# Recurrent chunks as a software pipeline: half levels of two directions in alternation, the neighbours' products between them

## The reference

```python
def step(S, inp):
    w_t, k_t, v_t, a_t, b_t = inp[-5:]
    sa = jnp.einsum('bhvk,bhk->bhv', S, a_t)
    S = S * w_t[:, :, None, :] + sa[..., None] * b_t[:, :, None, :] + v_t[..., None] * k_t[:, :, None, :]
    y_t = jnp.einsum('bhvk,bhk->bhv', S, inp[0]) if with_output else None
    return S, y_t
```

## Time and profile before

| | |
|---|---|
| median of 3 runs | 2862.22 us (2860.71 to 2863.34) |
| profiled execution | 2870.04 us, span 2868.2 us, granted clock 0.932 |
| PE busy | 2480.3 us (86%) |
| DVE / ACT / POOL busy | 1480.2 / 907.8 / 207.8 us |
| "rwkv chunks" of layer 0 | about 525 to 737 us of the span |
| "rwkv chunks" of layer 1 | about 1259 to 1464 us of the span |

### The profile page before, as it was taken

How to read it: one execution, slowest core, us unless ns; L and a number is a source line. 1 busy time by engine, 2 the same in 40 slices (tenths; PEclk the granted TensorE clock), 3 DMA queues, 4 the chain that set the end, 5 groups by cost and what they waited for, 6 DMA issues and landing times. The chain is left out here.

```text
span 2868.2 us, 48007 instructions
## 1 busy us (share of the span) xinstructions
PE 2480.3 (86%) x19670; PEld 1950.1 (68%) x19670; DVE 1480.2 (52%) x2429; ACT 907.8 (32%) x1473; POOL 207.8 (7%) x348
## 2 busy tenths in 40 slices
PE   7999989588588988958868988899999897899997
PEld 5776667488476765838756665678878566588785
DVE  4355522677736553256764676455542555555423
ACT  3234432111233344121114555322222354322221
POOL 0000000444000000035400000000000000000000
PEclk9999998799799999969979999899999999899998
DMA  8611111000021111200003211223333312233332
GB/s 280 228 45 30 30 45 48 2 3 4 9 59 46 58 37 37 70 1 4 3 12 100 59 52 45 66 74 95 96 89 95 94 52 73 59 95 95 93 93 70
DMA packets 299967, 182.50 MB, mean 64 GB/s; under 512 B 5226, under 2 KB 284412, under 8 KB 299660
## 3 DMA queue, kind: packets, MB, share of 16 engines
q1 hardware_dynamic: 286364, 150.50, 18.0%
q10 hardware_dynamic: 12480, 25.17, 2.5%
q0 software_dynamic: 944, 4.26, 0.4%
HBM read 177.79 MB, written 2.12 MB: 63 GB/s over the span
## 5 line engine op out<-in xcount | busy, mean ns | idle before, releaser
L245 DVE TENSOR_TENSOR wlo<-wraw,whi 128x1024 fp32r<-128x1024 f32 (+1 forms) x276 | 333.7, 1209 | 512.5 <-ACT whi L238 492.1
L306 PE MATMUL PW<-hhi,whi 128*128 128x512 f32 (+1 forms) x1152 | 433.7, 376 | 63.4 <-DVE hlo L991 41.2
L307 PE MATMUL PW<-hhi,wlo 128*128 128x512 f32 (+1 forms) x1152 | 432.6, 376 | 0.0
L308 PE MATMUL PW<-hlo,whi 128*128 128x512 f32 (+1 forms) x1152 | 432.1, 375 | 0.0
L238 ACT ACTIVATE whi<-wraw 128x1024 fp32r<-128x1024 f32 (+1 forms) x276 | 287.5, 1043 | 271.4 <-PE PW L308 256.0
L306 PEld LDWEIGHTS PW<-hhi,whi 128*128 128x128 f32 x1152 | 220.0, 191 | 105.8 <-issue 51.9
L308 PEld LDWEIGHTS PW<-hlo,whi 128*128 128x128 f32 x1152 | 219.8, 191 | 38.9
L307 PEld LDWEIGHTS PW<-hhi,wlo 128*128 128x128 f32 x1152 | 220.0, 191 | 38.2
L394 PE MATMUL PW<-hhi,whi 128*128 128x512 f32 (+1 forms) x592 | 221.3, 374 | 5.3 <-DVEq L2658 3.1
L396 PE MATMUL PW<-hlo,whi 128*128 128x512 f32 (+1 forms) x592 | 206.7, 349 | 0.0
L395 PE MATMUL PW<-hhi,wlo 128*128 128x512 f32 (+1 forms) x592 | 206.6, 349 | 0.0
(11 more groups left out here) (418 smaller groups left out, 4527.7 us busy)
## 6 DMA issues: line engine op xcount, KB each, us to landing
wraw<-in_w_in SPq DMA_DIRECT2D x68, 512.0 KB, 3.8
mod_w<-in_mod_w ACTq DMA_DIRECT2D x12, 2048.0 KB, 10.5
wraw<-in_ffn_w_gate SPq DMA_DIRECT2D x44, 512.0 KB, 3.8
wraw<-in_ffn_w_up SPq DMA_DIRECT2D x44, 512.0 KB, 3.8
wraw<-in_ffn_w_down SPq DMA_DIRECT2D x32, 512.0 KB, 3.7
wraw<-in_attn_w_in SPq DMA_DIRECT2D x24, 512.0 KB, 3.6
wraw<-in_w_out SPq DMA_DIRECT2D x16, 512.0 KB, 3.7
wraw<-in_rg_w_in SPq DMA_DIRECT2D x16, 512.0 KB, 3.8
```

Source lines behind the costliest of these rows:

```text
L245: dve.tensor_tensor(wlo[:, slot, 0:kb, :], wraw[:, slot, 0:kb, :], whi[:, slot, 0:kb, :].bitcast(F32), ALU.subtract).then_inc(S("w_split"), 1)
L306: pe.matmul(acc, whi[:, u % 2, k, :], rhi[:, k0 + k, s0:s1], start=a, stop=False)
L307: pe.matmul(acc, wlo[:, u % 2, k, :], rhi[:, k0 + k, s0:s1], start=False, stop=False)
L308: last_mm = pe.matmul(acc, whi[:, u % 2, k, :], rlo[:, k0 + k, s0:s1], start=False, stop=b)
```

## The change

The phase is written anew as a list of jobs that PE, ACT and DVE each walk in the same order (`program`, made by `slot`).

- A slot s holds the six levels of batch s. A level is split by direction: `p1` (T = MB X, 8 instructions, over four quadrants) and `p23` (the additions to X and to its transpose, 16 instructions of one direction). In order: P1 of direction 0, P23 of direction 1 of the level before, P23 of direction 0, P1 of direction 1.
- The level mask now has the identity in it, MB has the identity added, and the products give the whole new X and transpose at once; ACT copies both into XX (`act_X`, 512 columns), where DVE added before.
- Jobs of the batch behind (xa, gq, own and chain twice) and ahead (Lb, Lk, ab, kw) stand between the half levels: xa in level 0, gq in 1, the first step ("own") in 2, the second ("chain") in 3, Lb in 3, Lk in 4, ab and kw in 5. Lb waits for `y_added` of the batch behind. MB, MK and AW have two buffers; MK's and AW's second lie in slot 1 of the weight buffers, which are idle in this phase.
- The own parts and the chain accumulate in one bank: PE waits for its own `owned` signal between them. DVE then adds once per direction, and y in two operations.
- AW's first half comes from a product with the identity in 64x64 blocks; BK's two scaled halves are transposed in `ab` and `kw`, beside it and beside the W1 products.
- POOL makes A, K and B of both directions, then R, then the scaled parts. The chunk-end decays come from an ACT exponential (`act_ends`) where POOL copied them.
- Slot -1 prepares batch 0, slot 6 finishes batch 5.

```diff
--- before.py
+++ after.py
@@ -77,7 +77,7 @@
             r, c = t[:, None] >> j, s[None, :] >> j
             same = (r >> 1) == (c >> 1)
             lev.append(same & ((r & 1) == 1) & ((c & 1) == 0) if d == 0 else same & ((r & 1) == 0) & ((c & 1) == 1))
-    put("level", np.concatenate(lev, 1))
+    put("level", np.concatenate([m | (t[:, None] == s[None, :]) for m in lev], 1))
...
-            MB = arena2(f"MB{l}", [P, 8, 3, CH], off=38 * K1)
-            MK = arena2(f"MK{l}", [P, 8, 2, CH], off=44 * K1)
-            AW = arena(f"AW{l}", [P, 8, 2, CH], off=54 * K1)
+            MB = [arena2(f"MB0{l}", [P, 8, 3, CH], off=38 * K1), arena(f"MB1{l}", [P, 8, 3, CH], off=66 * K1)]
+            MK = [arena2(f"MK0{l}", [P, 8, 2, CH], off=44 * K1), place(f"MK1{l}", [P, 8, 2, CH], at=at_whi1)]
+            AW = [arena(f"AW0{l}", [P, 8, 2, CH], off=54 * K1), place(f"AW1{l}", [P, 8, 2, CH], at=at_wlo1)]
...
+            XX = arena(f"XX{l}", [P, 8, 2, CH], off=60 * K1)
...
+            def quarters(ds=(0, 1)):
+                for d in ds:
+                    for hp in range(2):
+                        for e_, pi in ((0, 0), (1, 1), (0, 1), (1, 0)):
+                            yield d, hp, e_, pi, 4 * d + 2 * hp + e_, half(e_), half(pi), half(pi ^ e_)
...
+            def pe_p1(e, j, lv, d):
+                if lv == 0 and d == 0:
+                    wait(e, mb, 1, j, 1)
+                if lv:
+                    wait(e, X_out, 12, j, 2 * lv - 1 + d)
+                if j or lv or d:
+                    wait(e, T_out, 12, j, 2 * lv + d)
+                for d_, hp, e_, pi, dh, re, rp, tp in quarters((d,)):
+                    ins = e.matmul(bank(e_)[tp, hp * CH:(hp + 1) * CH], MB[j % 2][rp, dh, 0, :],
+                                   XX[rp, inner(d, hp, e_), 1, :] if lv else ident2[rp, :], start=True, stop=True)
+                ins.then_inc(T_made.sem, 1)
+            def pe_p23(e, j, lv, d):
+                wait(e, T_out, 12, j, 2 * lv + d + 1)
+                if j and lv == 0:
+                    wait(e, X_out, 12, j - 1, 11 + d)
+                at = lambda c: PW[1 + d][:, c:c + CH]
+                new = lv == 0
+                def p2(hp, e_, pi):
+                    i, tp = inner(d, hp, e_), half(pi ^ e_)
+                    return e.matmul(at(384 + 128 * e_ + CH * hp)[half(pi), :], ident2[tp, :] if new else XX[tp, i, 0, :],
+                                    Tt[tp, i, :], start=True, stop=True)
+                def p3(hp, e_, pi):
+                    i, tp = inner(d, hp, e_), half(pi ^ e_)
+                    return e.matmul(at(128 * e_ + CH * hp)[tp, :], Tt[tp, i, :], ident2[tp, :] if new else XX[tp, i, 0, :],
+                                    start=True, stop=True)
+                for hp in range(2):
+                    for pi in range(2):
+                        if lv < 5:
+                            p2(hp, 1, pi)
+                        ins = p3(hp, 0, pi)
+                    for pi in range(2):
+                        if lv < 5:
+                            p2(hp, 0, pi)
+                        ins = p3(hp, 1, 1 - pi)
+                ins.then_inc(X_made.sem, 1)
...
+            def pe_scores(e, j, i):
+                if i == 0:
+                    for d in range(2):
+                        wait(e, AR_made, 2, j, d + 1)
+                    if j >= 2:
+                        wait(e, y_added, 1, j - 2, 1)
+                    elif j:
+                        wait(e, kw_out, 1, j - 1, 1)
+                else:
+                    wait(e, mb, 1, j, 1)
...
+            def pe_turned(e, j, i):
+                T = [order[d][j] for d in range(2)]
+                if i == 0:
+                    wait(e, mk, 1, j, 1)
+                    for d in range(2):
+                        wait(e, BK_made, 2, j, d + 1)
+                else:
+                    wait(e, ab_out, 1, j, 1)
+                for d, hp, e_, pi, dh, re, rp, tp in quarters():
+                    a = (2 * d + hp) * CH
+                    if i == 0:
+                        e.matmul(bank(6 + e_)[tp, a:a + CH], AR[re, d, hp, 0, rp], ident2[re, :], start=True, stop=True)
+                    else:
+                        e.matmul(bank(6 + e_)[tp, a:a + CH], MK[j % 2][rp, dh, 0, :],
+                                 vtok[rp, T[d], (2 * hp + e_) * CH:(2 * hp + e_ + 1) * CH], start=True, stop=True)
+                for d in range(2):
+                    for hp in range(2):
+                        ins = e.transpose(bank(6 + d)[:, 256 + hp * P:256 + (hp + 1) * P], BK[:, d, hp, 2 + i, :], ident)
+                ins.then_inc((turned_ab, turned_kw)[i].sem, 1)
...
+                ins.then_inc(owned.sem, 1)
+                wait(e, owned, 2, j, step + 1)
+                if j and step == 0:
+                    wait(e, state, 2, j - 1, 2)
+                for four in chunk():
+                    for what in range(2 if has_y(j) else 1):
...
+            def act_X(a, j, lv, d):
+                wait(a, X_made, 12, j, 2 * lv + d + 1)
+                src = PW[1 + d][:, 0:768].rearrange("p (x g b) -> p x g b", x=2, b=CH)[:, :, 0:4, :]
+                dst = XX[:, 4 * d:4 * d + 4].rearrange("p g x b -> p x g b")
+                if lv == 5:
+                    src, dst = src[:, 0], dst[:, 0]
+                a.activation(dst, src, ACT.Copy).then_inc(X_out.sem, 1)
...
+                    L = M[:, :, 0, :]
+                    ins = v.tensor_tensor(L, L, ident2.unsqueeze(1).to_broadcast([P, 8, CH]), ALU.add)
...
+            def slot(s):
+                back, ahead = s - 1, s + 1
+                jobs = {(0, 0): [("xa", back)], (1, 0): [("gq", back)], (2, 0): [("own", back), ("r_decays", ahead)],
+                        (3, 0): [("chain", back), ("ends", ahead)], (3, 1): [("Lb", ahead)], (4, 1): [("Lk", ahead)],
+                        (5, 0): [("ab", ahead), ("decays", ahead + 1)], (5, 1): [("kw", ahead)]}
+                here = 0 <= s < NBATCH
                 for lv in range(6):
...
+                    if here:
+                        yield "p1", s, lv, 0
+                        if lv:
+                            yield "p23", s, lv - 1, 1
+                    for name, j in jobs.get((lv, 0), ()):
+                        if 0 <= j < NBATCH:
+                            yield name, j, 0, 0
+                    if here:
+                        yield "p23", s, lv, 0
+                        yield "p1", s, lv, 1
+                        if lv == 5:
+                            yield "p23", s, 5, 1
+                    for name, j in jobs.get((lv, 1), ()):
+                        if 0 <= j < NBATCH:
+                            yield name, j, 0, 0
...
```

More of the change, by code:

```diff
@@ new lines, in pe_xa @@
+            def pe_xa(e, j):
+                wait(e, kw_out, 1, min(j + 1, NBATCH - 1), 1)
+                for d in range(2):
+                    wait(e, X_out, 12, j, 11 + d)
+                for d, hp, e_, pi, dh, re, rp, tp in quarters():
+                    a = (2 * d + hp) * 2 * CH
+                    ins = e.matmul(bank(6 + e_)[rp, a:a + 2 * CH], XX[tp, inner(d, hp, e_), 0, :], AW[j % 2][tp, dh, :, :],
+                                   start=True, stop=True)
+                ins.then_inc(xa.sem, 1)
@@ new lines, in pe_gq, with own @@
+            def pe_gq(e, j):
+                wait(e, xa_out, 1, j, 1)
+                for d, hp, e_, pi, dh, re, rp, tp in quarters():
+                    a = (2 * d + hp) * 2 * CH
+                    ins = e.matmul(bank(6 + pi)[re, a:a + 2 * CH], AW[j % 2][rp, dh, 1, :], MB[j % 2][rp, dh, 2:0:-1, :],
+                                   start=True, stop=True)
+                ins.then_inc(gq.sem, 1)
+            def own(d, hp, pi, re, what):
+                a = 4 * CH * what + (2 * d + hp) * CH
+                return bank(6 + pi)[re, a:a + CH]
@@ L1621, in pool_batch, with act_r_decays, act_ends @@
-            def pool_batch(g, j):
+                    a.activation(BK[:, d, :, 0, :], cum[:, d, :, s], ACT.Exp, scale=-1.0).then_inc(decays.sem, 1)
+            def act_r_decays(a, j):
+                if j >= 2 and has_y(j - 2):
+                    wait(a, QT_out, 1, j - 2 - first_y, 1)
+                for d in range(2):
+                    a.activation(AR[:, d, :, 1 + j % 2, :], cum[:, d, :, tiles(j)[d]], ACT.Exp).then_inc(r_decays.sem, 1)
+            def act_ends(a, j):
+                if j >= 2:
+                    wait(a, state, 2, j - 2, 2)
+                for d in range(2):
+                    c = 48 + 8 * (j % 2) + 4 * d
+                    end = tiles(j)[d].start + (CH - 1 if d == 0 else 0)
+                    a.activation(sm[:, c:c + 4].rearrange("p (i h) -> p h i", i=2), cum[:, d, :, end:end + CH + 1:CH],
+                                 ACT.Exp).then_inc(ends.sem, 1)
@@ new lines, in act_xa, with gq_part, act_G @@
+            def act_xa(a, j):
+                wait(a, xa, 1, j, 1)
+                for e_ in range(2):
```

(8 more changed lines are left out.)

440 lines of the change are left out of this document (180 added, 260 removed).

## The result

The changed kernel takes 2873.97 us (median of 9 runs, 2869.09 to 2885.71) against 2863.34 (9 runs of the kernel before beside it): ratio 1.004, 95% interval 1.0023 to 1.0058. The forecast was 2842, faster at 0.72. 2874 lies in the range given (2800 to 2878), on the wrong side of no change, and outside the 2815 to 2860 of the likeliest case. The profiled execution took 2873.79 us.

The account below looks back on a forecast made before the run. PE, or the chain through it, was taken to bound the 12 recurrent batches. Gains of 9.2 us in layer 0 and 11.4 in layer 1, together 20.6, off 2862.2 gave 2842 us; range 2800 to 2878.

Parts of the forecast that it names:

- the likeliest case: Whole kernel: the forecast of 2842 us itself, given 62%, with its own range 2815 to 2860.
- P23 of one direction: Half level on PE: 16 instructions over four quadrants take 0.70 us, bounds 0.46 and 0.93, plus 0.25 to the reader.
- own with its wait: First inter-batch step on PE, level 2: 32 instructions in 0.93 us, then PE waits for itself about 0.3.
- The rival on rates: P1 and P23 run at the old rate, 0.48 and 0.93 us: 3.1 us a slot, total 2877; 10%.
- the ledger: Term-by-term timeline of one slot (a batch's inversion with its neighbours' jobs): 29.5 us against 32.65 a batch before.
- T(0,4) behind Lb's masks: Level 4: DVE masks Lb from 19.1 to 21.2 ahead of T(0,4), so P23 starts at 21.7; wait 2.0 us.
- Lb behind y: Level 3: Lb waits until DVE has added y at 17.95 us of the slot, then runs to 18.8.
- Slot 0: the step that failed: Layer 0's first slot: POOL binds, Lb waits for AR(1) until 562.0, 11.6 us more to kw's end at 573.6.
- The rival on the clock: Long waits within slots halve the clock: both falling gives 2880 us, 10%; only one gives 2861, 12%.
- Start: Preparation of batch 0, uncovered sequential steps at half clock: 25.6 us in layer 0, 24.0 in layer 1.
- Steady slots: Slots 1 to 4: 29.5 us each, 118.0 in layer 0; 26.5, 26.5, 29.5, 29.5, 112.0 in layer 1.
- Slot 5 and the end: Last batch with no jobs ahead: X ends at 24.6 us, then xa through y until 36.5, in each layer.

Follow-up runs that it names:

- the sequence: The changed kernel without its interleaving: each batch's levels first, then all its jobs one behind the other; 3022.91 us, ratio 1.0552 to the kernel before.
- the warm start: The changed kernel with products nobody reads before the first scores and behind batch 0's Lb, Lk and ab; 2866.19 us, ratio 0.9989 to the kernel before.

## Why the prediction was wrong

**What held.** P23 of one direction took 0.70 us from its first load to its last (619.13 to 619.83), own with its wait 1.3 (619.77 to 621.09), the chain 0.8 (to 621.85). P1's 16 records begin within 0.22 us (0.35 less the last load's own 0.13). The rival on rates is out: four quadrants that share two banks run side by side. The rule weighed in the prediction, that different row tiles can't access the same PSUM bank simultaneously (the Trainium skill, TensorEngine Tiling (Array Packing), "Gotcha 1: PSUM Pressure"), doesn't agree with P1's row: with one row half at a time in each of the two banks the 16 would take 8 x 0.058 = 0.46 us. The waits came where the ledger put them, T(0,4) behind Lb's masks and Lb behind y. POOL did not bind in slots 1 to 4. The steady slot of layer 0 with almost no pause (slot 4, 0.3 us) took the ledger's 29.5.

**Slot 0: the step that failed.** "In slot 0, which has no jobs of a batch behind, POOL does bind" and "from Lb to kw's end are 11.6". POOL didn't bind there (Lb was issued with no wait), PE's levels did, at the half clock; only the 11.6 held (11.9). I gave the preparation the half clock of the stage's start and then took slot 0 at the full one. Nothing in the trace of before said that it would be back by then. The old stage also begins at the half clock, and there it was full after 3 us, with PE busy without a break (kernel before, columns as in the earlier trace rows):

```profile
541.00:543.00 2.00, 1.53 (x29) 1.56 (x33) 0.00 (x0) 0.00 (x0) 1.81 (x4) 0.50 0.00 0
543.00:545.00 2.00, 2.00 (x44) 1.83 (x38) 1.39 (x3) 0.00 (x0) 0.86 (x2) 0.57 0.03 8
545.00:547.00 2.00, 2.00 (x34) 1.83 (x34) 1.93 (x5) 1.09 (x2) 0.43 (x1) 1.00 0.00 0
```

The new preparation puts each step of PE behind a mask or a copy, and the levels of slot 0 have no jobs of a batch behind in them; the grant came back only at 569 and about 1300. A bare level costs 1.4 us more at that clock (the sequence's rows). The slot was 5.0 and 4.8 us over the ledger, of which the warm start took back 4.7 and 3.8 (23.0 and 22.3). Why the grant stays down so long isn't shown: by the records PE is as busy there (22.0 of 29.2 us) as in the steady slots, where it is 1.00. The rival on the clock looked in the wrong place, within the steady slots, where the grant is 1.00.

**Start.** 26.8 and 25.1 instead of 25.6 and 24.0: 1.2 and 1.1 us in sequential steps at 1.2 GHz that I priced a little low.

**Steady slots.** 3.8 and 4.1 us over the ledger's 118.0 and 112.0. The pauses are 4.4 and 3.7 us in the stages, 3.3 and 2.0 of them in slots 1 to 4, where before they were 2.2 and 2.3 in all; the remaining 0.5 and 2.1 us are not located. No term of the ledger had them: I took it that PE issues at the rate of the records as long as nobody makes it wait. With pauses put at the ledger's places, slot 2 fits: 1.0 us late from the second chain on, of which 0.6 is the pause at 627.80 in the chain and the rest its echo in T and the masks.

**Slot 5 and the end.** 39.0 and 41.7 instead of 36.5. In layer 0 1.2 us is a pause in the chain (until 719.18). In layer 1 1.7 us are pauses (the longer one, 1.4, from 1450.86), and the grant is half for 6.8 us (from 1453.4 and from 1463.6); how the 5.2 divide between these wasn't tested. In both layers PE waits there 1.5 for QT, 1.2 for AW and 1.6 for the last y one after the other, and I had about 0.5 us less for these hops.

Added, 12.6 and 15.3 us: from 20.6 faster to 7.0 slower in the stages' own rows. Slot 0 is 9.8 of these 27.9, the largest term and a third of the miss; the steady slots are 7.9, slot 5 and the end 7.7, the start 2.3. With slot 0 right, the rows would still say 2.8 faster and not 20.6, and the warm start came out at 0.9989, not at the forecast's 0.993: the pauses, which the ledger put at nothing, and the end fell away from it too. The runs' ratio (1.004) is 11 us; the 4 between, and whatever differs outside the stages, are not located. The sign was lost by terms of 1 to 5 us, each at a place where the order of the work was new. My chance of 0.72 rested on a ledger whose slots had only costs known from a busy, warm PE; every term that it lacked was a cost.

## What to carry to other kernels

When a rewrite takes PE's work away, price the time also at the lower granted clock wherever PE stands or works thinly, first of all at a stage's start; products that nobody reads, put where PE waits anyhow, gave 0.3% in the old order and 0.5% in the new. A pipeline of very short instructions can run PE out of instructions (here a packet with some 125 records of PE came every 3.2 us at best): count the records in the dense stretches and look for idle time with no releaser. Measure an interleaving against its own sequence and not only against the old kernel, since it has first to win back what its pieces cost.

## What the hardware did that I had not expected

- Pauses of PE of 0.2 to 1.8 us with no wait, each of the 189 ending 1.19 to 1.61 us after the end of a 16 KB packet of the instruction queue: 4.4 us in layer 0's stage with 5616 records in 201.6 us, 11.4 with 6768 in 221.9, 1.5 with 5760 in 222.5, none with the changed kernel's 5616 spread over 275.5.
- The grant stayed at 0.50 for 29 us although PE was busy 22 of these by the records, with 494 of them; ten unread products of 512 columns ahead of them and nine of 256 between them had it at 1.00 there but for 3.4 us.
- Records of different quadrants run past each other at the full rate even where four of them share two banks: 16 begin within 0.22 us.
